# A hybrid decoder layer on eight cores: bf16 weight copies stored one block later, final norm reordered at the very end

## The reference

```
h   = rms_norm(x, ln_mix_g) @ w_in                    # 1024 -> 2560
y_a = rms_norm(spatial_gating(h[:, :1024]), grp_norm_a)
y_b = rms_norm(short_gated_conv(h[:, 1024:]), grp_norm_b)
x   = x + concat(y_a, y_b) @ w_out
x   = x + cross_attention(rms_norm(x, ln_attn_g), memn, w_q, w_kv, w_o)
g,u = split(rms_norm(x, ln_ffn_g) @ w_gate_up)        # 1024 -> 2 x 2816
x   = x + (silu(g) * u) @ w_down                      # 2816 -> 1024
return rms_norm(x, ln_final_g)    # x * rsqrt(mean(x*x) + 1e-6) * ln_final_g
```

## Time and profile before

| | |
|---|---|
| median of 3 runs | 1647.4 us (1646.38 to 1668.82) |
| profiled execution, its own time | 1647.78 us |
| span of its slowest core (core 4) | 1646.2 us |
| spans of the cores | 1630.2 to 1646.2 us |
| PE busy | 1586.7 us, 96% |
| DVE, ACT, POOL busy | 57%, 43%, 5% |
| DMA by POOL's queue (q0) | 122.95 MB |
| DMA by SP's queue (q1) | 161.26 MB |

### The profile page before, as it was taken

How to read it: one execution, slowest core, us unless ns; L and a number is a source line. 1 busy time by engine, 2 the same in 40 slices (tenths; PEclk the granted TensorE clock), 3 DMA queues, 4 the chain that set the end, 5 groups by cost and what they waited for, 6 DMA issues and landing times.

```text
span 1646.2 us, 22268 instructions; the slowest of 8 cores (1630.2 to 1646.2 us)
## 1 busy us (share of the span) xinstructions
PE 1586.7 (96%) x7679; PEld 752.5 (46%) x7820; DVE 942.3 (57%) x1501; ACT 707.3 (43%) x1280; POOL 76.0 (5%) x152
## 2 busy tenths in 40 slices
PE   5998989999999999999999999999999999999997
PEld 2454444444444444444444444444444444444456
DVE  4777773247455565636654565874778557743324
ACT  4654745124475246543564335343444345431221
POOL 2000000010000100000000000000000000000000
PEclk9999999999999999999999999999999999999999
DMA  9696848879997999788867995668755575424741
GB/s 216 112 181 145 196 83 138 138 136 208 220 221 127 160 230 237 175 152 178 249 187 174 167 235 188 215 131 187 201 188 192 139 162 202 154 87 157 260 162 52
DMA packets 44349, 285.64 MB, mean 174 GB/s; under 512 B 4944, under 2 KB 6992, under 8 KB 21200
## 3 DMA queue, kind: packets, MB, share of 16 engines
q0 software_dynamic: 20032, 122.95, 44.0%
q1 hardware_dynamic: 24208, 161.26, 27.7%
HBM read 365.20 MB, written 38.27 MB: 245 GB/s over the span
## 4 chain that ended last, share of the span: by engine, by line
PE 89%; DMA 7%; issue 1%; ACT 1%; DVE 1%; DVEq 0%; POOL 0%; SPq 0%; ACTq 0%; POOLq 0%
PE ps L620 63%; PE ps L1425 16%; PE ps L1134 7%; PE ps L1413 2%; DMA big<-w_gate_up 2%; DMA big<-w_v 1%; DMA big<-gu 1%; DMA big<-w_qT 1%; DMA big<-w_down 1%; DMA big<-w_vu 1%; DMA big<-w_cv 1%; PE ps L696 0%; DMA big<-fold 0%; DVE big L750 0%; PE ps L1186 0%
## 5 line engine op out<-in xcount | busy, mean ns | idle before, releaser
L620 PE MATMUL ps<-big 128*128 128x512 bf16 (+1 forms) x5176 | 1150.0, 379 | 25.4 <-DMA big<-w_vu 5.2
L620 PEld LDWEIGHTS ps<-big 128*128 128x128 bf16 x5280 | 517.5, 98 | 632.4 <-issue 39.0
L668 ACT ACTIVATE big<-big 128x512 f32<-128x512 f32 (+1 forms) x320 | 192.2, 610 | 374.6 <-DVE big L946 247.3
L1425 PE MATMUL ps<-big 128*128 128x512 bf16 (+1 forms) x1404 | 276.7, 354 | 1.9 <-DMA big<-w_down 0.9
L1359 DVE TENSOR_TENSOR big<-ps,big 128x512 bf16<-128x512 f32 x176 | 120.0, 688 | 184.3 <-PE ps L620 139.3
L946 DVE TENSOR_TENSOR big<-ps,big 128x512 f32<-128x512 f32 x184 | 127.2, 691 | 164.0 <-PE ps L1425 83.8
L678 DVE TENSOR_TENSOR big<-big 128x512 f32<-128x512 f32 (+2 forms) x272 | 179.4, 667 | 57.5 <-ACT big L668 54.3
L750 DVE SCALAR_TENSOR_TENSOR big<-big 128x512 bf16<-128x512 f32 (+3 forms) x256 | 172.0, 722 | 49.1 <-ACT big L708 32.9
L1425 PEld LDWEIGHTS ps<-big 128*128 128x128 bf16 x1424 | 139.0, 98 | 133.0 <-issue 1.8
L1353 ACT ACTIVATE big<-ps 128x512 f32<-128x512 f32 x176 | 102.6, 594 | 208.8 <-PE ps L620 199.3
L1134 PE MATMUL ps<-big 128*128 128x512 bf16 x499 | 114.3, 379 | 1.6 <-DVE big L946 0.9
(11 more groups left out here) (90 smaller groups left out, 627.8 us busy)
## 6 DMA issues: line engine op xcount, KB each, us to landing
big<-gu SPq DMA_DIRECT2D x56, 1024.0 KB, 6.6
big<-w_gate_up POOLq DMA_DIRECT2D x32, 1024.0 KB, 11.4
big<-fold SPq DMA_DIRECT2D x28, 1024.0 KB, 7.4
big<-w_down POOLq DMA_DIRECT2D x36, 704.0 KB, 8.4
big<-w_cv POOLq DMA_DIRECT2D x28, 768.0 KB, 8.4
big<-dn SPq DMA_DIRECT2D x28, 704.0 KB, 4.8
big<-w_out POOLq DMA_DIRECT2D x14, 1024.0 KB, 11.7
y<-big SPq DMA_DIRECT2D x7, 2048.0 KB, 10.8
```

What stands on the lines that cost most here:

```text
L620: ins = e.matmul(b, lhsT=ws[k], rhs=rs[k], start=(k == 0), stop=(k == nk - 1))
L668: act((lambda e: e.activation(out=sq, in_=src, func=AF.Square)), [src], [sq], Tn)
L1425: ins = e.matmul(b, lhsT=w[:, k, :], rhs=hb[:, k, lo:hi], start=(k == 0), stop=(k == KF - 1))
```

## The change

Groups are stored to DRAM one block later than before, so each group is a cast for one block more (19 more casts and 19 fewer copies in all; the 19 stores stay). In the last block's final norm the sum of squares is kept in two parts: seven chunks on DVE, whose sum goes through one matmul, and the eighth square, which is made in bf16 and added by a second matmul into the same bank. The norm's weight is applied to each chunk in place by itself (`gain`), and the factor is then applied by three DVE instructions over 3, 3 and 2 chunks, each followed by its store.

```diff
         for k in range(11):
-            p = 1 + k % 3
+            p = 2 + k % 3
             R2.groups.append(("cast" if i <= p else "copy", w_gu_d[k] if i <= p else k, (2, 8, 256), k, i == p))
         for k in range(8 if i < NS - 1 else 0):
-            p = 3 + k % 2
+            p = 4 + k % 2
             R2.groups.append(("cast" if i <= p else "copy", w_dn_d[k] if i <= p else 11 + k, (KF, 128), 11 + k, i == p))
...
-            n = Norm(8, 3)
+            n = Norm(7, 3)
+            box = {}
             for m in range(8):
...
-                n.add(xm, 256)
+
+                def gain(m=m, xm=xm):
+                    g = cvec[:, C_FIN + m:C_FIN + m + 1]
+                    dve((lambda e: e.tensor_scalar(out=xm, in0=xm, scalar1=g, scalar2=None, op0=ALU.mult)), [xm, cvec],
+                        [xm], 256)
+
+                def square16(xm=xm, box=box):
+                    box["f"] = sq_bufs.get()
+                    sq = box["s"] = box["f"].bitcast(BF16)[:, 0:256]
+                    act((lambda e: e.activation(out=sq, in_=xm, func=AF.Square)), [xm], [sq], 256)
+
+                def sum7(n=n):
+                    n.bank = banks.get()
+                    b7 = banks.ap(n.bank)[:, 0:256]
+                    o = n.out[:, 0:256]
+                    pe((lambda e: e.matmul(b7, lhsT=ones, rhs=o, start=True, stop=False)), [ones, o],
+                       [banks.ap(n.bank)], mm_cost(1, 256), "ones")
+                    acb_bufs.put(n.out)
+
+                def sum8(n=n, box=box):
+                    b7 = banks.ap(n.bank)[:, 0:256]
+                    sq = box["s"]
+                    pe((lambda e: e.matmul(b7, lhsT=ones, rhs=sq, start=False, stop=True)), [ones, sq],
+                       [banks.ap(n.bank)], mm_cost(1, 256), "ones")
+                    sq_bufs.put(box["f"])
+                if m < 7:
+                    n.add(xm, 256)
+                else:
+                    n.th.put("act", square16, [xm], 256, sq_bufs)
+                    n.th.put("pe", sum7, lambda n=n: [n.out], 0.11, banks)
+                    n.th.put("pe", sum8, lambda box=box: [box["s"]], 0.11)
+                n.th.put("dve", gain, [xm], 256)
+            n.onpe = True
             n.rstd(D, 256)
...
+            for c0, c1 in ((0, 3), (3, 6), (6, 8)):
+                def part(n=n, lo=lo, c0=c0, c1=c1):
+                    src = xt(i)[:, c0:c1, lo:lo + 256]
+                    sd = n.sd
+                    dve((lambda e: e.tensor_tensor(out=src, in0=src, in1=sd.unsqueeze(1).to_broadcast([128, c1 - c0, 256]),
+                                                   op=ALU.mult)), [src, sd], [src], (c1 - c0) * 256)
+                    out_dmas.append(S.add("sp", (lambda e: e.dma_start(out=y_d[:, i, c0:c1, lo:lo + 256], in_=src)),
+                                          reads=[src], dma_key=("yl", lo, c0), cost=(c1 - c0) * 131072 / 330e3))
+                    if c1 == 8:
+                        std_bufs.put(n.sdf)
+                n.th.put("dve", part, lambda n=n: [n.sd], (c1 - c0) * 256)
```

More of the change, by code:

```diff
@@ L1440, in last_down @@
                 banks.put(bi)
-                n.add(xm, 256)
-            n.rstd(D, 256)
[L1443 to L1449, removed]
+                def gain(m=m, xm=xm):
+                    g = cvec[:, C_FIN + m:C_FIN + m + 1]
+                    dve((lambda e: e.tensor_scalar(out=xm, in0=xm, scalar1=g, scalar2=None, op0=ALU.mult)), [xm, cvec],
+                        [xm], 256)
```

## The result

Over 21 runs of each in alternation the changed kernel takes 1663.5 us at the median against 1647.4, ratio 1.0116 [1.0091, 1.0141]: 19 us slower by the ratio. Some executions of every kernel here are longer at a lower granted clock; medians contain them, and ratios leave out those over 1.5% above the fastest, so that three of the changed kernel's at 1683 to 1686 us are still in its ratio. The forecast was 1646.1 us with a range to 1657; the time is outside it, beyond the rival that ended slower (B, 1657.3). The profiled execution's slowest core spans 1666.1 us, 19.9 more than before.

What follows compares the result with a forecast made beforehand. TensorE was taken as the bound, with DMA close behind in blocks 1 and 2 alone. -5.9 + 5.0 - 0.52 + 0.11 = -1.3 took the profiled 1647.8 to 1646.5, forecast as 1646.1 us; likeliest 1643 to 1650, range 1638 to 1657.

Steps and rivals of the forecast that it cites:

- B: Rival: DMA becomes the bound in block 2 from a share of 1, 16.2 in place of 5.0; 1657.3 us, chance 0.12.
- Block 1, -5.9: Block 1 without its four gate/up stores: waits of 5.0 us on gate/up and 0.9 on down weights go.
- The other order, 0 within 2 us: Scheduler may order the streams another way; TensorE's work is the same, so 0, within 2 us either way.
- Block 2, +5.0: Block 2's gate/up phase, four copies become casts: a wait like block 1's old one, +5.0 us; bounds 0 and 16.2.
- Block 4, 0: Block 4 at a DMA share of 0.83, below the 0.92 borne without a wait: 0; bounds -3.7 and +5.0.
- Blocks 3 and 5, 0: Blocks 3 and 5 at DMA shares of 0.86 and 0.67, below the 0.92 borne without a wait: 0.
- Price of a cast, 6.2 against 3.0: A gate/up group costs all 16 DMA engines 6.2 us as a cast, 3.0 as a copy or store.
- A: Rival: block 2 swallows its casts without a wait; 1641.1 us, or 1637.4 with block 4's wait gone too; chance 0.27.
- D: Rival: block 1's late cast was due to the store of y beside it and stays; 1652.0 us, chance 0.11.
- C: Rival: DVE holds off the casts' descriptors, one wait of 5.0 in each of blocks 2 to 4; 1656.1 us, chance 0.03.
- The queues, 0: POOL's and SP's in-order queues: the same waits one block later, covered by the ring's three slots, 0.
- The end: Final norm: matmul starts earlier, -0.52 us; one more matmul, +0.11; drain of stores sets the end, so scales give 0.

Runs made afterwards that it cites:

- e4: Kernel before the change, its DMAs and old end kept, but with the engine orders the scheduler makes for e1_weights; 1651.2 us, ratio 1.0026.
- e3: Kernel before the change with the later stores and copies, but its engine orders and old end kept; 1673.1 us, ratio 1.0166.
- e13: e1_weights with 40 idle matmuls put right ahead of block 2's late gate/up group; ratio 1.0104.
- e9: e1_weights with the four gate/up casts added to block 2 reading a same-size bf16 tensor; 1651.9 and 1654.7 us, two executions.
- e15: e1_weights with the two w_out casts ahead of block 2's late cast made plain DMAs from a bf16 tensor; ratio 1.0035.
- e1_weights: Kernel before the change with only the later stores and copies, old end kept; 1662.6 us, ratio 1.0100.

## Why the prediction was wrong

- **Block 1, -5.9**: right in the time, and by little. The wait on w_gate_up near 428 is gone on every core, and the DMA share fell to 0.85 as computed. But the casts did not land "near 9 to 11": their median is 14.5 (DMA issues, 360 to 530 us) against 15.5 before, and the late cast of that place, issued at 401.4, still took 22.9 us, which is 0.8 less than the 23.7 that had covered it before:

```profile
big<-w_gate_up POOLq DMA_DIRECT2D x1, 1024.0 KB, 22.9
```

- **The other order, 0 within 2 us**: wrong on the slowest core. ACT stood behind a load of x in block 1, 2.9 + 1.7 us here, and TensorE waits 1.6 us on DVE behind block 4's late cast. That second wait is of the order too: it is 3.2 us in e4, which has no such cast there, and absent in e3.
- **Block 2, +5.0**: this is the step that failed. "Nearest is the row of block 1, which has exactly that list of DMAs: +5.0." The list was the same, and so was the landing, 26.4 us against 27.1. But a wait is the landing less the work that covers it, and I never looked at the cover in block 2. It is two groups of 6.9 us and little else, 15 us, where in block 1 about 10 us of other matmuls stood between, 24 us. The step measured 12.6, 7.6 more than the sum had. e13 shows that cover takes the wait away; e9 and e15 show what fills the landing.
- **Block 4, 0**: failed in the same way. I compared a mean share (0.83 forecast, 0.78 measured) with what block 2 had borne. The late cast shares 21 us with a load of x, a fold load and a w_vu cast, and has 13 us of cover: 7.8 + 2.9, where the copy in that place had cost 3.7. That is 7.0 more than the sum had, as much as block 2's miss, and above the bound of +5.0. Of the 21.2 us between the forecast and the profiled core these two steps are 14.6, and the order 6.2.
- **Blocks 3 and 5, 0**: right for feed-forward weights, on which no core of the changed kernel waits there. Block 3 has a new wait of 0.5 to 2.1 us on ACT near 845 to 863 on seven cores; in its chain stands again a load of x that ACT's squares wait for.
- **Price of a cast, 6.2 against 3.0**: right on the average (49.6% for 140.26 MB is again 5.9 us a MB), and the 53 us of added DMA time too (56 by the shares of the two queues). But it is no price of a single late cast, which waits out its queue.
- **Rival B** had the right direction for the wrong reason: it made the share of 1 the point from which DMA decides. The share stayed at 0.93 and the waits came all the same. Its upper end for block 2, 16.2, held; none was given for block 4 beyond +5.0. **A** fell, and **D** too, though the late cast of block 1 is nearly as late as D had it. **C** is not needed: e15 explains the long landings without DVE; no run tried C itself.
- **The queues, 0**: POOL's waits on gate/up stores (53.6 us) and on down stores (10.6) are no longer in sum than the 85.3 before. That the cast, though issued at once, would land behind w_out's, is what this step did not ask.
- **The end**: -0.53 against -0.52, the drain unchanged. The three parts are there and change nothing.

## What to carry to other kernels

When a copy becomes a cast, or any transfer slower, take its landing time at its own place, with what is ahead in its queue, and set against it the engine's work between the freeing of the buffer and its use at that place. A mean share of DMA time, or a twin with the same transfers elsewhere, doesn't tell this. Where prefetch is a ring of few slots, these runs speak for slow transfers at places where other work stands between its groups, and against two slow transfers close together in one queue; and a copy that pays for later blocks is worth storing as early as the DMA engines bear it.

## What the runs showed that was not expected

In nearly every execution one core of each pair (0 and 1, 2 and 3, 4 and 5, 6 and 7) is ahead of the other, whichever of the two, mostly by 9 to 15 us in the changed kernel, by 6 to 13 in the one before and by 3 to 9 in e4. In one execution of the changed kernel 1659.0 and 1646.6, 1648.2 and 1659.3, 1641.5 and 1655.3, 1658.2 and 1647.4. In e1_weights the core behind has a wait of 9.9 to 11.1 us in block 2 where its partner has 5.1 to 6.5 in every pair; in the changed kernel the late cast lands in 25.8 and 26.4 us on cores 4 and 6 and in 21.5 and 22.6 on 5 and 7. The runs don't say what the pair shares; no experiment tried it.

In the last half block, the residual add at 1649.70 waited for the first stores of y of the other half:

```profile
1649.70 0.42 DVE L1440 TENSOR_TENSOR big<-ps,big 128x256 f32<-128x256 f32 x1 [1.85 <-DMA y<-big]
```

The scheduler's dependences go by the hull of a strided piece of x, so a store of three chunks of one half claims the other half's bytes between them. DVE had caught up before the last chunk, so no cost of it is seen here.
